# Attention heads taken in pairs on the row halves of the array, values as the stationary operand on column halves, layer norm weights applied on VectorE

## The reference

```python
h = rms_norm(x, n1) * (1.0 + sc1) + sh1
proj = h @ w_in                       # q 512, k 128, v 128, convolution 1024 columns
q, k = rms_norm(q, qg), rms_norm(k, kg)    # 8 query heads, 2 key/value heads of 64; rotary on latent tokens
s = einsum('bqhgd,bkhd->bhgqk', q, k) * scale
attn = einsum('bhgqk,bkhd->bqhgd', softmax(s), v)
conv = silu(layer_norm(depthwise_conv31(a * sigmoid(b)) + dw_b, ln_g, ln_b))
x = x + g1 * (concat([attn, conv]) @ w_out)
h2 = rms_norm(x, n2) * (1.0 + sc2) + sh2
x = x + g2 * grouped_moe(h2, ...)     # top 1 group of 4, top 2 experts in it
```

## Time and profile before

| what | value |
|---|---|
| time, median of 3 runs | 1123.59 us (1122.86 to 1124.43) |
| profiled execution | its span is 1121.9 us; no time of its own is given |
| TensorE busy | 982.3 us, 88% of the span |
| VectorE busy | 404.9 us, 36% |
| ScalarE, GpSimd busy | 157.1 us, 123.3 us |
| bytes moved | 328.59 MB |

### The profile page before, as it was taken

The page is one execution under the profiler, slowest core; times in us unless marked ns, Lnnn a source line. Parts: engine busy times, 40 slices in busy tenths (PEclk is TensorE's granted clock), DMA queues, the critical chain, the costliest instruction groups (busy, mean ns, idle before and its releaser), DMA issues. The chain is left out here.

```text
span 1121.9 us, 12453 instructions
## 1 busy us (share of the span) xinstructions
PE 982.3 (88%) x4812; PEld 467.2 (42%) x4812; DVE 404.9 (36%) x902; ACT 157.1 (14%) x364; POOL 123.3 (11%) x188
## 2 busy tenths in 40 slices
PE   4799999997898989988799979999678997889886
PEld 2555545454333333333266544554523333333332
DVE  0189855245211110111435994533521111011206
ACT  1101233220000000000130014422000000000010
POOL 1001200511000000000221020060200000000010
PEclk9899889997999999988799997999579999999988
DMA  9928973368999996999950475225965999999932
GB/s 339 383 95 310 302 298 108 124 219 355 424 420 425 425 367 272 422 427 421 360 220 24 150 270 223 76 92 185 362 234 220 415 426 425 423 424 422 420 134 75
DMA packets 64570, 328.59 MB, mean 293 GB/s; under 512 B 7448, under 2 KB 10184, under 8 KB 48084
## 3 DMA queue, kind: packets, MB, share of 16 engines
q1 hardware_dynamic: 44224, 277.89, 61.6%
q0 software_dynamic: 9072, 27.89, 6.8%
q10 hardware_dynamic: 11172, 21.42, 5.8%
HBM read 305.88 MB, written 21.30 MB: 292 GB/s over the span
## 5 line engine op out<-in xcount | busy, mean ns | idle before, releaser
L1782 PE MATMUL ps<-big 128*64 128x512 f32 x1024 | 244.6, 630 | 27.6 <-issue 11.9
L1798 PE MATMUL ps<-big,scr 128*64 128x512 f32 x624 | 156.3, 644 | 5.6 <-DVE scr L1428 4.3
L1477 PE MATMUL ps<-big 128*128 128x384 f32 (+2 forms) x448 | 147.9, 492 | 5.1 <-ACT big L786 5.1
L1782 PEld LDWEIGHTS ps<-big 128*64 128x64 f32 x1024 | 78.5, 144 | 173.1 <-issue 159.5
L1124 DVE SCALAR_TENSOR_TENSOR scr<-scr,convw 128x384 f32<-128x384 f32 x240 | 134.1, 613 | 2.3
L1441 DVE TENSOR_TENSOR scr<-ps,scr 128x256 f32<-128x256 f32 x32 | 13.6, 424 | 278.2 <-ACT scr L953 278.1
L1477 PEld LDWEIGHTS ps<-big 128*128 128x128 f32 x448 | 86.0, 193 | 64.7 <-issue 24.8
L1798 PEld LDWEIGHTS ps<-big,scr 128*64 128x64 f32 x624 | 50.6, 148 | 97.9 <-issue 96.9
L1698 PE MATMUL ps<-big 128*128 128x512 f32 x192 | 84.4, 594 | 1.4 <-ACT big L826 1.4
L1493 PE MATMUL ps<-big,cs_rep 128*32 128x256 f32 x640 | 49.5, 466 | 14.4 <-DMA big<-in_w_mod_dram 14.4
L953 ACT ACTIVATE scr<-ps 128x256 f32<-128x256 f32 x32 | 12.3, 383 | 325.2 <-PE ps L1782 325.2
(11 more groups left out here) (231 smaller groups left out, 842.5 us busy)
## 6 DMA issues: line engine op xcount, KB each, us to landing
big<-in_w_gate_dram SPq DMA_DIRECT2D x32, 2048.0 KB, 18.4
big<-in_w_up_dram SPq DMA_DIRECT2D x32, 2048.0 KB, 22.8
big<-in_w_down_dram SPq DMA_DIRECT2D x32, 2048.0 KB, 18.9
big<-in_w_mod_dram SPq DMA_DIRECT2D x23, 2048.0 KB, 15.3
big<-in_w_in_dram SPq DMA_DIRECT2D x6, 2048.0 KB, 23.5
expert_rows<-scr ACTq DMA_DIRECT2D x68, 128.0 KB, 8.5
big<-in_w_out_dram SPq DMA_DIRECT2D x4, 2048.0 KB, 19.8
expert_rows<-x ACTq DMA_DIRECT2D x1, 7168.0 KB, 42.6
```

Source lines behind the costliest of these rows:

```text
L1477: mm = pe.matmul(out, stationary(k), moving(k), start=(k == 0), stop=(k == n - 1))
L1782: mm = pe.matmul(ps[b * TT:(b + 1) * TT, bank, :].rearrange("p (m n) -> p m n", m=2), tokens(k), w[:, :, k, b * HF:(b + 1) * HF], start=(k ...
L1798: mm = pe.matmul(ps[b * TT:(b + 1) * TT, bank, :], src[:, k % 2 * P + k // 2 * TT:k % 2 * P + (k // 2 + 1) * TT], w[:, k, b * SEG:(b + 1) ...
```

## The change

Attention now runs over twelve units `u`: pair `j = u // 3` holds the two query heads `j` and `4 + j`, one of each key/value head, and `t = u % 3` is the tile. The two heads' score matmuls stand next to each other, on rows 0 to 63 and 64 to 127 of the array, in different banks. The probabilities are now divided by their row sum before they are transposed: VectorE takes the inverse (`inverse_sum`) and GpSimd multiplies (`share`). The values are stationary, 64 columns for each head, and write output that is already transposed, so ScalarE copies it straight to where the output projection reads it (`take_attention`), and `head_output` and the first three `mix_transposed` go. To fit this layout the attention rows of `w_out` are loaded by two transfers of 64 partitions, the rest by a third.

VectorE's program in attention is written anew: per unit the maximum of the next unit, the taps given by `UNIT_TAPS`, the inverse sum. The fills are spread by `UNIT_FILL`. The layer norm's weight and bias are applied on VectorE in two `scalar_tensor_tensor`, which also normalize, and GpSimd keeps the inverse deviation and the last product. Two of the three `conv_back` move ahead of the last unit's transposes. One wait on `ov_taken` is added in the experts' part, behind expert 0.

```diff
+LOGITS = [7, 4, 7]
+UNITS = PAIRS * TILES
+SCORE_BANK = [3, 5]
+BACK = [3, 4, 5]
...
+UNIT_TAPS = [1, 4, 4, 1, 4, 4, 1, 4, 3, 0, 0, 0]
...
+UNIT_FILL = [1, 2, 2, 1, 2, 2, 1, 2, 2, 1, 0, 0]
...
-        prob = scr[:, 0:TILES * 384].rearrange("p (t n) -> p t n", t=TILES)
-        probT = scr[:, TILES * 384:2 * TILES * 384].rearrange("p (t n) -> p t n", t=TILES)
+        prob, probT = (scr[:, n * 4 * 384:(n + 1) * 4 * 384].rearrange("p (b g n) -> p b g n", b=2, g=KV_HEADS)
+                       for n in range(2))
...
+        w_out_v = w_out[:, QW:MIX, :].rearrange("l (k p) n -> l p k n", p=P)
+        w_out_heads = w_out[:, 0:QW, :].rearrange("l (g j d) n -> l g d j n", g=KV_HEADS, d=HD)
...
+                    item, cols = ("out", l, n), slice(n * SEG, (n + 1) * SEG)
+                    s = slot_of(item)
+                    if past(uses(item) - 1):
+                        sp.wait_ge(slot_used[s], uses(item) - 1)
+                    for g_ in range(KV_HEADS):
+                        sp.dma_start(slot_w(s)[g_ * HD:(g_ + 1) * HD, 0:PAIRS, :], w_out_heads[l, g_, :, :, cols])\
+                            .then_inc(slot_loaded[s], 16)
+                    sp.dma_start(slot_w(s)[:, PAIRS:KD, :], w_out_v[l, :, :, cols]).then_inc(slot_loaded[s], 16)
...
                         if l:
                             halos()
 
-                pool.wait_ge(mod_taken, taken_at(l, 2))
-                lane_out(pool, mod_dram[:, 2 * D:3 * D], rowC, modC_st)
-                pool.wait_ge(modC_st, (l + 1) * LANES * 16)
-                spread(gateB[:, :, :], 2, bcG_in)
-
...
+                def share(u):
+
+                    n = P * len(KEY_CHUNKS[u % TILES])
+                    p_ = prob[:, u % 2, :, 0:n]
+                    pool.wait_ge(rinv_ready, l * UNITS + u + 1)
+                    g.tensor_tensor(p_, p_, stats(RI + 2 * (u % 2), 2).unsqueeze(2).broadcast_to([P, 2, n]), ALU.mult)\
+                        .then_inc(prob_ready, 1)
+
+                pool.wait_ge(qkT_ps, l * 4 + 4)
+                pool.dma_start(gainB, norm2_g[l:l + 1, :].broadcast_to([2, D]).rearrange("p (a n) -> p a n", a=2))\
+                    .then_inc(gain_in, 16)
+                for u in range(UNITS):
+                    share(u)
+                    if u == 1:
+                        pool.wait_ge(mod_taken, taken_at(l, 2))
+                        lane_out(pool, mod_dram[:, 2 * D:3 * D], rowC, modC_st)
+                    if u == 5:
+                        pool.wait_ge(modC_st, (l + 1) * LANES * 16)
+                        spread(gateB[:, :, :], 2, bcG_in)
...
+                for t in range(TILES):
+                    pool.wait_ge(ln_var, l * 3 + t + 1)
+                    rstd(stats(LNR + t), stats(LNV + 2 * t + 1), 1, 1.0, EPS).then_inc(ln_rstd, 1)
                 pool.wait_ge(cache_st, l * 32 + 32)
...
                     pool.wait_ge(ln_sig, l * 3 + t + 1)
                     g.tensor_tensor(h[:, t, CH:D], h[:, t, CH:D], sg, ALU.mult).then_inc(mix_ready, 1)
...
+                def softmax(u):
+
+                    n = P * len(KEY_CHUNKS[u % TILES])
+                    act.wait_ge(nmax, l * UNITS + u + 1)
+                    for g_ in range(KV_HEADS):
+                        at = 2 * (u % 2) + g_
+                        ins = a.activation(prob[:, u % 2, g_, 0:n], ps[:, SCORE_BANK[u % 2] + g_, 0:n], ACT.Exp,
+                                           bias=stats(NM + at), accum_out=stats(RS + at))
+                    ins.then_inc(exp_done, 1)
+
+                def take_probT(u):
+                    n = P * len(KEY_CHUNKS[u % TILES])
+                    act.wait_ge(t_ps, l * UNITS + u + 1)
+                    a.copy(probT[:, u % 2, :, 0:n], ps[:, 1:3, 0:n]).then_inc(probT_ready, 1)
+
+                def take_attention(j):
+
+                    act.wait_ge(o_ps, l * PAIRS + j + 1)
+                    a.copy(hT_all[:, :, j, :], by_seg(ps[:, 7, 0:CAP])).then_inc(attn_out, 1)
...
+                softmax(0)
+                for u in range(UNITS):
+                    if u + 1 < UNITS:
+                        softmax(u + 1)
+                    take_probT(u)
+                    if u and u % TILES == 0:
+                        take_attention(u // TILES - 1)
+                take_attention(PAIRS - 1)
                 for t in range(TILES):
...
+                def score_max(u):
...
+                    at, n = SCORE_BANK[u % 2], P * len(KEY_CHUNKS[u % TILES])
+                    dve.wait_ge(s_ps, l * UNITS + u + 1)
+                    v.tensor_reduce(stats(NM + 2 * (u % 2), 2), ps[:, at:at + 2, 0:n], AX.X, ALU.max, negate=True)\
+                        .then_inc(nmax, 1)
...
+                def inverse_sum(u):
+
+                    at = 2 * (u % 2)
+                    dve.wait_ge(exp_done, l * UNITS + u + 1)
+                    v.reciprocal(stats(RI + at, 2), stats(RS + at, 2)).then_inc(rinv_ready, 1)
...
                     step.link(v.bn_stats(stats(BN, 6), ps[:, BACK[t], :]))
...
+                    v.bn_aggr(stats(LNV + 2 * t, 2), stats(BN, 6)).then_inc(ln_var, 1)
...
                 def ln_normalize(t):
+
+                    z = h[:, t, CH:D]
+                    if t == 0:
+                        dve.wait_ge(ln_in, (l + 1) * 32)
+                    dve.wait_ge(ln_var, l * 3 + t + 1)
+                    step.link(v.scalar_tensor_tensor(z, ps[:, BACK[t], :], stats(LNV + 2 * t), lnB[:, 0, :],
+                                                     ALU.subtract, ALU.mult))
                     dve.wait_ge(ln_rstd, l * 3 + t + 1)
-                    v.tensor_scalar(h[:, t, CH:D], ps[:, BACK[t], :], stats(LNV), stats(LNR), ALU.subtract, ALU.mult)\
-                        .then_inc(ln_norm, 1)
+                    v.scalar_tensor_tensor(z, z, stats(LNR + t), lnB[:, 1, :], ALU.mult, ALU.add).then_inc(ln_out, 1)
...
+                score_max(1)
+                for u in range(UNITS):
+                    if u == 5:
+                        mod_take(l, 8)
+                    if u:
+                        if u + 1 < UNITS:
+                            score_max(u + 1)
+                    taps(UNIT_TAPS[u])
+                    inverse_sum(u)
+                    if u == 10:
+                        mod_take(l, 9)
+                for t in range(TILES):
+                    ln_stats(t)
+                for t in range(TILES):
+                    ln_normalize(t)
...
+                def scores(u):
...
                     ks = KEY_CHUNKS[t]
...
+                    for g_ in range(KV_HEADS):
+                        rows = slice(g_ * HD, (g_ + 1) * HD)
+                        mm = pe.matmul(ps[:, SCORE_BANK[u % 2] + g_, 0:P * len(ks)], qT[rows, t, j * P:(j + 1) * P],
+                                       kT[rows, ks[0] * P:(ks[-1] + 1) * P], start=True, stop=True)
+                    mm.then_inc(s_ps, 1)
+
+                def prob_transposed(u):
+                    for g_ in range(KV_HEADS):
+                        for n in range(len(KEY_CHUNKS[u % TILES])):
+                            mm = pe.transpose(ps[:, 1 + g_, n * P:(n + 1) * P], prob[:, u % 2, g_, n * P:(n + 1) * P], ident)
+                    mm.then_inc(t_ps, 1)
+
+                def weighted_values(u):
+                    j, t = divmod(u, TILES)
+                    ks = KEY_CHUNKS[t]
+                    pe.wait_ge(probT_ready, l * UNITS + u + 1)
+                    if t == 0 and past(l * PAIRS + j):
+                        pe.wait_ge(attn_out, l * PAIRS + j)
+                    for n, c_ in enumerate(ks):
+                        for g_ in range(KV_HEADS):
+                            mm = pe.matmul(ps[g_ * HD:(g_ + 1) * HD, 7, (TILES - 1 - t) * P:(TILES - t) * P],
+                                           vall[:, c_, g_ * HD:(g_ + 1) * HD], probT[:, u % 2, g_, n * P:(n + 1) * P],
+                                           start=(n == 0), stop=(n == len(ks) - 1))
+                    if t == TILES - 1:
+                        mm.then_inc(o_ps, 1)
 
...
+                scores(0)
+                scores(1)
+                for u in range(UNITS):
+                    pe.wait_ge(prob_ready, l * UNITS + u + 1)
+                    if u == 0:
+                        pe.wait_ge(mod_taken, taken_at(l, 3))
+                    else:
+                        pe.wait_ge(probT_ready, l * UNITS + u)
+                    prob_transposed(u)
+                    if u + 2 < UNITS:
+                        scores(u + 2)
+                    if u:
+                        weighted_values(u - 1)
+                    unit_fill(l, u)
+                    if u == UNITS - 2:
+                        conv_back(0)
+                        conv_back(1)
+                conv_back(2)
+                weighted_values(UNITS - 1)
...
+                    pe.wait_ge(mix_ready, l * 3 + t + 1)
+                    if t == 0:
...
+                        k = PAIRS + m
```

(10 more changed lines are left out.)

199 lines of the change are left out of this document (46 added, 153 removed).

## The result

The changed kernel takes 1148.17 us (median of 4 runs, 1144.99 to 1149.91), the kernel before on the same chip 1124.01 us. Its ratio is 1.0219 with a 95% interval of 1.0171 to 1.0267: slower, by 24.6 us on 1123.6; whether by more than 2% the interval leaves open. The forecast was 1166 with a range of 1137 to 1191. Sign and mechanism came as forecast, the size did not: it was put 18 us too high.

The account below looks back on a forecast made before the run. TensorE was taken to bound attention before the change, a closed loop after it. Per layer 10.5 + 12.2 - 1.3 = 21.4 us, for two 42.8, on 1123.6 gives 1166 us; range 1137 to 1191.

Parts of the forecast that it names:

- The chain that the new order makes: Attention: each unit's work stands one behind the other in a closed loop; 10.5 us longer a layer at full clock.
- The ring of waits: Attention's closed loop: transposes, scores, maximum, taps, inverse sum, GpSimd's multiplication, next transposes; steps summing to 62.8 us a layer.
- TensorE's work: Attention: transposes, scores, weighted values, fill and convolution back of all twelve units take 40 us a layer at full clock.
- S: Attention's scores of two heads, row halves working at once: 0.84 us with 384 columns, 0.41 with 128.
- W: Attention's weighted values per unit: 0.95 us for a latent tile, between 0.66 and 1.4, and 0.3 for tile 0.
- The clock: Attention: TensorE's idle stretches in the loop bring half clock for part of the time, costing 12.2 us a layer.
- step 4 to 5: Attention, from unit 4's to unit 5's transposes: the take of the first fill half waits for the fill; 10.1 us.
- all at half clock: Attention's upper sum for the clock: everything on the loop at half clock costs 24.4 us more a layer.
- The rival at full clock: Attention keeps full clock nearly throughout, so only the loop costs: 18 us more, 1142 us; chance 0.17.
- I credit all 1.3: Output projection: the new layer norm removes TensorE's whole idle time waiting for GpSimd's normalization, 1.3 us a layer.
- The rest: Outside attention: layer norm gives 1.3 us a layer; three transfers cost nothing; the expert wait nothing, at most 1 us.
- TensorE stays the bound: Attention: VectorE and GpSimd keep ahead, 50.5 us a layer, both layers gain 24, 1099 us; chance 0.12.

Follow-up runs that it names:

- experiment 1: Changed kernel with VectorE's inverse sum moved to the start of each unit's step, ahead of maximum and taps; ratio to the kernel before 0.9876.
- experiment 5: Changed kernel with only the taps moved behind the inverse sum on VectorE; ratio to the kernel before 0.9982.
- Experiment 7: Changed kernel with 10 to 28 small matmuls, results unused, in each of TensorE's waits to hold the clock up; ratio to the kernel before 1.0203.
- experiment 3: Changed kernel with both score matmuls of a unit on the lower row half, one after the other; ratio to the kernel before 1.0576.
- experiment 4: Kernel before with only the layer norm edit and the three transfers per output projection slot; ratio to the kernel before 0.9964.
- Experiment 9: Kernel with inverse sum first and four rope taps, plus mix transposes earlier in the output projection; 1092.46 us, ratio to the kernel before 0.9754.
- experiment 2: Changed kernel with each unit's multiplication moved from GpSimd to VectorE, behind the inverse sum; ratio to the kernel before 1.0214.

## Why the prediction was right, and where its size was wrong

**The chain that the new order makes: right.** The ring of waits is the one written down, and experiments 1 and 5 show it by opening it. Forecast steps at full clock were 6.7, 6.2, 4.35, 7.1, 10.1, 4.4, 7.1, 6.0, 4.35, 4.5, 2.0. Experiment 7, which has full clock, gives 6.1, 5.6, 4.3, 6.4, 9.5, 4.3, 6.4, 5.3, 4.3, 4.0, 2.2 once the ends of the small matmuls are taken off. Every step is in its place, and those that hold a large multiplication are 0.5 to 0.7 us too long in the forecast, mostly because the multiplication of 768 columns takes 1.47 us, not 1.9. I had scaled 1.27 us for 512 columns in proportion; 610 and 1468 ns for 256 and 768 columns make a line with some 0.18 us that do not grow with the columns, and by it 512 would take 1.04, less than the 1.27 of a row with other operands. Seven times 0.43 are 3.0 us. Another 0.9 lies ahead of the first transposes (4.4 us in experiment 7, forecast 5.3). Attention at full clock was 66.3, not 71.8 us: 5.5 too high a layer, 11.0 in all.

**TensorE's work: right.** S of two heads is 0.84 and 0.43 (experiment 3). W is 0.81 from start to start (156.38 to 157.19), where I took 0.95 between 0.66 and 1.4.

**The clock: the term that was mis-sized most.** I wrote that half of 24.4 us would be lost, "I take half: 12.2". It is 6.0 and 4.8 us. Half clock does come with the long waits, as argued, but it covers little of what stands on the loop: mostly one unit's transposes (1.54 in place of 0.87 for six) and scores (0.3 to 0.7 us longer), and it is gone in a unit that follows without a wait (154.73: six transposes in 0.87). It does not come behind every wait at once: behind the 3.41 us ahead of 190.03 six transposes still took 0.88, and only the fill behind them was at half clock (3.55 at 191.62). Work at half clock that ends inside a wait costs nothing: behind the fill at 151.02 (3.37 us in place of 1.9) the transposes still wait 0.34 us for GpSimd. The fill at 168.27 is of the other kind, since the take waits for it: its 1.4 us are part of the 2.6 by which step 4 to 5 is longer in layer 0 (12.1) than in layer 1 (9.5), where it ran at full clock. The sum "all at half clock" counted only what lies on the loop, but "half of it" was a guess with no row behind it. 6.8 us a layer on average: this is the larger part of the miss. The rival at full clock, 1142, came nearer than the forecast, but not for its reason: attention was shorter than its sum by 5.5 us and longer by 5.4 us of clock.

The reading of the earlier trace rows behind it was wrong as well. The clock was not back "from the fill at 144.40 on": those four records took 3.57 us, and at full clock four take 1.88 (166.13 in the earlier trace rows). It was back behind them, at 147.7, in the weighted values:

```profile
147.90 1.77 PE L1477 MATMUL ps<-scr 128*128 128x64 f32 x14
```

So TensorE had worked without a gap since 133.02, for over 14 us, before it had full clock.

**"I credit all 1.3" for the layer norm: failed.** Together with the three transfers, on the kernel before, it gives 0.8 (experiment 4). In the changed kernel the projection is longer by 1.8 and 0.2 us. Its rows in layer 0, TensorE first, then ScalarE:

```profile
221.05 7.13 PE L1737 MATMUL ps<-big 128*128 128x512 f32 x16 [0.68 <-ACT big L845]
...
229.30 10.57 PE L1737 MATMUL ps<-big 128*128 128x512 f32 x24 [0.67 <-ACT big L845]
...
248.53 1.16 PE L1580 MATMUL ps<-table_sb,big 128*128 128x128 f32 x8 [1.37 <-DVE big L1094]
```
```profile
240.34 0.59 ACT L845 COPY big<-ps 128x512 f32<-128x512 f32 x1 [11.09 <-PE ps L1720]
240.34 0.39 ACTq L748 DMA_DIRECT2D scr<-in_b_mod_dram  x1
...
243.83 1.06 ACT L786 ACTIVATE big<-x 128x1024 f32<-128x1024 f32 x1 [2.90 <-issue]
```

Two groups of transposes stand directly ahead of the half product that needs ScalarE's copy of them: 0.68 and 0.67 us. The third is late, and in layer 0 ScalarE issues eight transfers behind its copy, from 240.34 to 243.8; the square sum behind them is late, the normalization that it feeds too, and TensorE waits 1.37 us. Both are in the diff, in the new order of mix_transposed, and I had read only how long the layer norm takes and not what the moved transposes are followed by. Experiment 9 takes both away.

**The rest: right as far as shown.** The three transfers cost nothing that experiment 4 can show, which has them only together with the layer norm.

**The sum.** 42.8 forecast, less 13.6 for the clock (10.8 in place of 24.4), less 11.0 for the loop, plus 4.6 for the projection (2.0 lost in place of 2.6 gained), is 22.8, against 24.6 measured. The rest lies outside attention and projection, mostly in the experts, where its cause is open. The projection's 4.6 us went the other way than the two large errors, and by luck the total missed by less for it.

**The rival "TensorE stays the bound"** was worked out at 50.5 us of attention and 1099 us. Experiment 1 comes near that world: 49 us, and 0.9876, or 1110 from 1123.6. It needed one line of the order. I had priced the multiplication as the thing that decides; the taps weigh more.

**What would show it:** waits in the named places, seen; units of 6 to 7 us, seen; one near 10, 12.1 and 9.5; granted clock 0.62 to 1.00, higher than the 0.6 to 0.9; attention "about 84", 71 to 72.

The Trainium skill's GPSIMD Engine Reference, section Engine selection, prefers VectorE for elementwise work with two inputs, GpSimd being about twice as slow. The 958 against 1468 ns of experiment 2 agree in direction, at 1.5 times. As a reason for the slowdown it fails: in experiment 1 GpSimd does the same multiplications and the kernel is fast.
